# RWKV-7 front of a decoder trunk: decay and rate ranks as column pairs from unmixed input, keys first, two wide POOL products on VectorE

## What is computed

```python
xx = jnp.pad(h[:, :-1], ((0, 0), (1, 0), (0, 0))) - h
mixed = h[None] + xx[None] * mu[:, None, None, :]
r, k, v = jnp.einsum('ibsd,ide->ibse', mixed[:3], w_rkv)
xw, xa, xg = mixed[3], mixed[4], mixed[5]
w_log = -jax.nn.softplus(-(w_dec0 + jnp.tanh(xw @ w_dec1) @ w_dec2).astype(f32)) - 0.5
decay = jnp.exp(-jnp.exp(w_log))
a = jax.nn.sigmoid((a0 + (xa @ a1) @ a2).astype(f32))
g = jax.nn.sigmoid(xg @ g1) @ g2
kk = heads(k * k_k)
kk = kk / jnp.maximum(jnp.sqrt(jnp.sum(kk * kk, axis=-1, keepdims=True)), 1e-12)
k_h = heads(k) * (1.0 + (a_h - 1.0) * k_a.astype(f32).reshape(RW_HEADS, RW_HEADSIZE))
o = rwkv7_scan(r_h, w_h, k_h, v_h, kk, a_h)
```

## Time and profile before

| | |
|---|---|
| time, three runs | 1217.82 us median (1216.81 to 1221.8) |
| profiled execution | 1216.76 us, its span 1215.0 us |
| mean granted TensorE clock | 0.969 |
| TensorE busy | 1150.2 us, 95% |
| VectorE busy | 431.4 us, 36% |
| ScalarE busy | 267.9 us, 22% |
| POOL busy | 93.5 us, 8% |

### The profile page before, as it was taken

The page is one execution under the profiler, slowest core; times in us unless marked ns, Lnnn a source line. Parts: engine busy times, 40 slices in busy tenths (PEclk is TensorE's granted clock), DMA queues, the critical chain, the costliest instruction groups (busy, mean ns, idle before and its releaser), DMA issues.

```text
span 1215.0 us, 15687 instructions
## 1 busy us (share of the span) xinstructions
PE 1150.2 (95%) x6523; PEld 762.4 (63%) x6523; DVE 431.4 (36%) x946; ACT 267.9 (22%) x439; POOL 93.5 (8%) x106
## 2 busy tenths in 40 slices
PE   4799999998989999999999799979999999999997
PEld 2686698984478844444445478838887844444455
DVE  0364654265720321111111484874423411111113
ACT  2222010414220311111111353323331311111113
POOL 5002221200000100000000001331000100000000
PEclk9899899999989899999999899998988999999999
DMA  9797765329967379959999630000069689999991
GB/s 352 262 331 276 277 229 187 138 98 381 402 238 266 121 292 385 387 201 369 387 386 340 246 104 35 1 0 2 2 218 390 223 306 386 387 387 386 387 383 42
DMA packets 157180, 309.56 MB, mean 255 GB/s; under 512 B 9568, under 2 KB 10940, under 8 KB 157116
## 3 DMA queue, kind: packets, MB, share of 16 engines
q1 hardware_dynamic: 156320, 307.39, 69.5%
q10 hardware_dynamic: 796, 1.23, 0.3%
HBM read 307.55 MB, written 1.05 MB: 254 GB/s over the span
## 4 chain that ended last, share of the span: by engine, by line
PE 86%; DVE 6%; SPq 2%; ACT 2%; DMA 1%; issue 1%; ACTq 1%; DVEq 0%
PE bank L1136 19%; PE bank L779 15%; PE bank L1160 10%; PE bank L840 7%; PE bank L1069 6%; PE bank L1061 6%; PE bank L790 2%; PE bank L906 2%; DVE scratch L2406 2%; PE bank L812 1%; PE bank L749 1%; PE bank L1193 1%; PE bank L1201 1%; PE bank L1372 1%; DVE scratch L2408 1%
## 5 line engine op out<-in xcount | busy, mean ns | idle before, releaser
L779 PE MATMUL bank<-arena,ring 128*128 128x256 f32 x960 | 211.5, 382 | 5.5 <-DMA ring<-in_ev_w_in 2.8
L779 PEld LDWEIGHTS bank<-arena,ring 128*128 128x128 f32 x960 | 182.8, 191 | 30.8 <-DMA ring<-in_ev_w_in 3.2
L1136 PE MATMUL bank<-ring,arena 128*64 128x512 f32 x704 | 153.7, 592 | 0.0
L1136 PEld LDWEIGHTS bank<-ring,arena 128*64 128x64 f32 x704 | 50.4, 137 | 99.6 <-issue 99.4
L2280 DVE TENSOR_TENSOR arena<-arena,bank 128x512 f32<-128x512 f32 x17 | 11.7, 688 | 220.7 <-PE bank L1136 220.7
L840 PE MATMUL bank<-arena,ring 128*128 128x256 f32 x384 | 86.1, 388 | 2.8 <-DVE arena L2504 2.8
L1069 PE MATMUL bank<-arena 128*128 128x256 f32 x336 | 83.1, 394 | 1.7 <-issue 1.7
L1136 PE MATMUL bank<-arena 128*64 128x512 f32 x384 | 84.1, 592 | 0.0
L840 PEld LDWEIGHTS bank<-arena,ring 128*128 128x128 f32 x384 | 74.8, 195 | 14.0 <-issue 3.2
L1061 PEld LDWEIGHTS bank<-arena 128*128 128x128 f32 x608 | 69.3, 192 | 13.8 <-issue 13.8
L1061 PE MATMUL bank<-arena 128*128 128x128 f32 x608 | 72.7, 278 | 0.0
(11 more groups left out here) (358 smaller groups left out, 1337.4 us busy)
## 6 DMA issues: line engine op xcount, KB each, us to landing
ring<-in_moe_w SPq DMA_DIRECT2D x112, 1024.0 KB, 14.2
arena<-in_moe_w SPq DMA_DIRECT2D x80, 1024.0 KB, 14.2
ring<-in_mod_w SPq DMA_DIRECT2D x24, 2048.0 KB, 11.0
ring<-in_ev_w_in SPq DMA_DIRECT2D x13, 2048.0 KB, 12.8
ring<-in_od_w_rkv SPq DMA_DIRECT2D x6, 2048.0 KB, 13.6
ring<-in_ev_w_out SPq DMA_DIRECT2D x4, 2048.0 KB, 17.1
ring<-in_od_w_o SPq DMA_DIRECT2D x2, 2048.0 KB, 10.7
arena<-in_x ACTq DMA_DIRECT2D x1, 1024.0 KB, 9.1
```

The costliest lines, as they stand in the source:

```text
L779: mm = pe.matmul(ps[:, c * S:(c + 1) * S], w_cols(slot)[:, k, (2 * half + c) * P:(2 * half + c + 1) * P], src[:, k, :], start=(k == 0), st ...
L1136: mm = pe.matmul(bank[4 + half][e * C:(e + 1) * C, :], hgT[:, kb, e * C:(e + 1) * C], piece(slots[e], kb), start=(kb == 0), stop=(kb == KB ...
```

## The change

- Decay and rate ranks: POOL scales the two 64-wide first weights with mu once their tile has landed. TensorE computes `h @ w + xx @ (mu * w)` for both, side by side in the two column halves of bank 4, one rank in partitions 0 to 63 and one in 64 to 127. The second products read row halves 0 to 63 and 64 to 127 and go to two banks (`decay_and_rate`). Their mixed inputs are no longer made; VectorE makes the four differences and mixes gate, key, receptance and value.
- The gate's first product stands between the second and third `decay_and_rate`, its second product behind the key projections and lengths. Keys are projected next after the ranks. Two of the four `key_products` stand within the first receptance tile.
- ScalarE does all four key evacuations, then all four roots, then the gate, then LT. The value mix stands ahead of the maxima on VectorE, when the key projections are done.
- The receptance products (L724, L729) go from POOL to VectorE, behind the second transpose of the solve.

```diff
+    FULL_RANKS = FULL_IN + 8
...
-                    srcs = [(wt[0:64, 0:D], t["od_w_dec2"][0]), (wt[0:64, D:2 * D], t["od_a2"][0]),
-                            (wt[:, 2 * D:3 * D], t["od_g2"][0])]
+                    srcs = [(wt[0:64, 0:D], t["od_w_dec2"][0]), (wt[64:P, 0:D], t["od_a2"][0]),
+                            (wt[:, D:2 * D], t["od_g2"][0])]
...
-                    sp.wait_ge(lora_full, 3)
+                    sp.wait_ge(lora_full, 2)
...
-                    sp.wait_ge(proj_full, FULL_LORA)
+                    sp.wait_ge(proj_full, FULL_LORA + 4)
...
-                    sp.wait_ge(proj_full, FULL_LORA + 2 * at + 2)
+                    sp.wait_ge(proj_full, (FULL_LORA if at >= 2 else FULL_RANKS) + 2 * at + 2)
...
-            pool.wait_ge(proj_full, FULL_LORA + 4)
+            _, slot, count = plan[1][places[1, "la"][0]]
+            pool.wait_ge(tile_landed[slot], 16 * count)
+            for i in range(2):
+                for k in range(KB):
+                    v = (i * KB + k) * HEAD
+                    ins = pool.tensor_scalar(weight(slot)[:, 2048 + v:2048 + v + HEAD], weight(slot)[:, v:v + HEAD],
+                                             col("od_mu", (3 + i) * KB + k), None, ALU.mult)
+            ins.then_inc(ranks_scaled, 1)
+            pool.wait_ge(proj_full, FULL_RANKS + 4)
...
-            pool.memset(buf(11), 0.0)
-            pool.wait_ge(rw_exp, 4)
-            pool.wait_ge(proj_evac, 26 + 12 + 8)
-            pool.tensor_tensor(AR[:, :, :, 1, :], by_tile(5), by_tile(10), ALU.mult).then_inc(r_ready, 1)
+            pool.memset(buf(11), 0.0).then_inc(kc_ready, 1)
...
-                if pr == 1:
-                    pool.wait_ge(r_ready, 1)
-                    pool.tensor_tensor(by_tile(10), AR[:, :, :, 1, :], rwK, ALU.mult).then_inc(r_ready, 1)
...
-                second = [wl[0:64, 0:D], wl[0:64, D:2 * D], wl[:, 2 * D:3 * D]]
-                rank = [64, 64, P]
-                for i in range(3):
+                second = [wl[0:64, 0:D], wl[64:P, 0:D], wl[:, D:2 * D]]
+                low = [slice(0, 64), slice(64, P)]
...
+                scaled_first = [wa[:, 2048 + 512 * i:2560 + 512 * i].rearrange("p (k n) -> p k n", k=KB)
+                                for i in range(2)]
...
+                for k in range(KB):
+                    if k % 2 == 0:
+                        pe.wait_ge(h_ready, 8 + k // 2 + 1)
+                    for i in range(2):
+                        pe.matmul(bank[4][low[i], 0:S], first[i][:, k, :], hT[:, k, :], start=(k == 0), stop=False)
+                pe.wait_ge(ranks_scaled, 1)
+                for k in range(KB):
+                    if k % 2 == 0:
+                        pe.wait_ge(diff_ready, k // 2 + 1)
+                    for i in range(2):
+                        mm = pe.matmul(bank[4][low[i], 0:S], scaled_first[i][:, k, :], xx[:, k, :],
+                                       start=False, stop=(k == KB - 1))
+                mm.then_inc(lora_full, 1)
...
+                def decay_and_rate(u):
...
+                    two_banks = (proj_bank(), proj_bank())
+                    for c in range(2):
+                        d = 2 * u + c
+                        for i in range(2):
+                            mm = pe.matmul(two_banks[i][:, c * S:(c + 1) * S], second[i][:, d * P:(d + 1) * P],
+                                           lora[0][low[i], :], start=True, stop=True)
+                            if c:
+                                mm.then_inc(proj_full, 1)
...
+                def gate_first():
...
-                        pe.wait_ge(mix_ready, i + 4 if i else k // 2 + 1)
-                        mm = pe.matmul(bank[4][0:rank[i], 0:S], first[i][:, k, :], mixed[i % 2][:, k, :],
+                        if k % 2 == 0:
+                            pe.wait_ge(mix_ready, k // 2 + 1)
+                        mm = pe.matmul(bank[5][:, 0:S], first[2][:, k, :], mixed[0][:, k, :],
...
-                    pe.wait_ge(lora_evac, i + 1)
...
+                def gate_second():
...
-                            mm = pe.matmul(ps[:, c * S:(c + 1) * S], second[i][:, d * P:(d + 1) * P],
-                                           lora[i][0:rank[i], :], start=True, stop=True)
+                            mm = pe.matmul(ps[:, c * S:(c + 1) * S], second[2][:, d * P:(d + 1) * P], lora[1],
+                                           start=True, stop=True)
...
+                pe.wait_ge(lora_evac, 1)
+                decay_and_rate(0)
+                decay_and_rate(1)
+                gate_first()
+                decay_and_rate(2)
+                decay_and_rate(3)
...
+                    src = mixed[(1, 0, 1)[n]]
...
+                pe.wait_ge(mix_ready, 5)
+                rkv(0, 0)
+                rkv(0, 1)
+                pe.wait_ge(lora_evac, 2)
+                early_lengths()
+                late_lengths()
+                gate_second()
+                pe.wait_ge(mix_ready, 6)
...
+                def early_products():
+                    pe.wait_ge(kk_max, 4)
+                    key_products(0)
+                    key_products(1)
...
+                rkv(1, 0, between=early_products)
+                key_products(2)
+                key_products(3)
+                rkv(1, 1)
...
-                rkv(0, 0)
-                rkv(0, 1, early_lengths)
-                pe.wait_ge(mix_ready, 8)
-                rkv(1, 0, late_lengths)
-                pe.wait_ge(kk_max, 4)
-                for j in range(4):
-                    key_products(j)
-                rkv(1, 1)
-                pe.wait_ge(mix_ready, 9)
...
-                        pe.wait_ge(kc_ready, pr + 1)
+                        pe.wait_ge(kc_ready, pr + 2)
...
-                lora_func = [ACT.Tanh, ACT.Copy, ACT.Sigmoid]
-                for i, (dst, bias) in enumerate(((sgT, "od_w_dec0"), (aT, "od_a0"), (ggT, None))):
-                    r = P if i == 2 else 64
-                    act.wait_ge(lora_full, i + 1)
-                    act.activation(lora[i][0:r, :], bank[4][0:r, 0:S], lora_func[i]).then_inc(lora_evac, 1)
-                    for u in range(4):
+                act.wait_ge(lora_full, 1)
+                act.activation(lora[0][0:64, :], bank[4][0:64, 0:S], ACT.Tanh)
+                act.activation(lora[0][64:P, :], bank[4][64:P, 0:S], ACT.Copy).then_inc(lora_evac, 1)
+                for u in range(4):
+                    for dst, bias in ((sgT, "od_w_dec0"), (aT, "od_a0")):
...
-                        if bias is None:
-                            ins = act.activation(dst[:, 2 * u:2 * u + 2, :].rearrange("p k s -> p (k s)"),
-                                                 bank[n % 4][:], ACT.Copy)
-                        else:
-                            for c in range(2):
-                                b = 2 * u + c
-                                ins = act.activation(dst[:, b, :], bank[n % 4][:, c * S:(c + 1) * S], ACT.Sigmoid,
-                                                     bias=col(bias, b))
+                        for c in range(2):
+                            b = 2 * u + c
+                            ins = act.activation(dst[:, b, :], bank[n % 4][:, c * S:(c + 1) * S], ACT.Sigmoid,
+                                                 bias=col(bias, b))
...
+                act.wait_ge(lora_full, 2)
+                act.activation(lora[1], bank[5][:, 0:S], ACT.Sigmoid).then_inc(lora_evac, 1)
...
-                evac_keys(0)
-                evac_keys(1)
-                evac_keys(2)
-                key_root(0)
-                key_root(1)
-                evac_keys(3)
-                key_root(2)
-                key_root(3)
-                evac_products(0)
-                evac_products(1)
-                evac_T(rT, 0)
-                evac_products(2)
-                evac_products(3)
+                for u in range(4):
+                    evac_keys(u)
+                for u in range(4):
+                    key_root(u)
+                evac_T(ggT, 0)
+                evac_T(ggT, 4)
+                for j in range(4):
+                    evac_products(j)
...
+                evac_T(rT, 0)
...
-                    i = (3, 4, 5, 1, 0, 2)[n]
+                    i, place = ((5, 0), (1, 1), (0, 0), (2, 1))[n]
...
-                        if n == 0 and b % 2 == 0:
-                            tt_(xx[:, b:b + 2, 1:S], hT[:, b:b + 2, 0:S - 1], hT[:, b:b + 2, 1:S], ALU.subtract)
-                            link(ts_(xx[:, b:b + 2, 0:1], hT[:, b:b + 2, 0:1], -1.0, None, ALU.mult))
-                        ins = stt(mixed[n % 2][:, b, :], xx[:, b, :], col("od_mu", i * KB + b), hT[:, b, :],
+                        ins = stt(mixed[place][:, b, :], xx[:, b, :], col("od_mu", i * KB + b), hT[:, b, :],
...
-                dve.wait_ge(h_ready, 12)
+                for q in range(4):
+                    dve.wait_ge(h_ready, 8 + q + 1)
+                    b = 2 * q
```

(50 more changed lines are left out.)

## The result

The changed kernel takes 1209.3 us (median of 9 runs; before 1217.8, 9 runs). One of its nine runs took 2005.74 us at a granted clock of 0.553 and is left out of the ratio. The ratio is 0.9919, 95% interval 0.9896 to 0.9942: 0.8% faster.

The account below looks back on a forecast made before the run. It took two nearly equal paths, TensorE's stream and the solve, to bound the front. An earlier loop start (-5.8) and the clock (-3.0) gave -8.8 from 1216.76: 1208.0 profiled, 1209 as median, range 1204 to 1217.

Parts of the forecast that it names:

- What bounds: Layer 1's front: TensorE's stream (813.6) and the solve (820.2) end within 6.7 us of each other.
- Ranks: Decay and rate rank matmuls, paired in column halves: 0.11 us a record, keys start 12.1 us earlier.
- The feared half microsecond at the sigmoids: ScalarE's sigmoids keep ahead of the banks by only 0.2 us; half a microsecond may be lost there.
- The rival that pairs don't overlap: Rank pairs don't run side by side: 0.216 us a record, +6.8, 1215.8 us; chance 0.10.
- the rival of weight loads in the open: Weight loads of the rank column pairs don't overlap matmuls: 0.353 us a record, +15.6, 1224.7 us; chance 0.05.
- The new wait: TensorE stands 6.5 us before the first receptance tile, until the gate copy behind four key roots; half clock costs 2.7 more.
- Part 3: Receptance products moved from POOL to VectorE: worth 5.8 us of the 8.4 us that two solve steps stood still.
- the first two parts: Part 1: paired decay and rate ranks, keys 12.1 us earlier. Part 2: keys first, loop may start 5.8 us earlier.
- The clock at the loop: Idle before the loop shrinks from 6.7 to 0.7 us, so its first pass keeps full clock: 3.0 us gained, at most 4.0.
- Sum: -5.8 for the loop's earlier start and -3.0 for the clock make -8.8: 1208.0 profiled, 1209 median.

Follow-up runs that it names:

- products_alone: The kernel before with only the two wide receptance products moved from POOL to VectorE, behind the second transpose; 1209.70 us, ratio 0.9929 to the kernel before.
- ranks_apart: The changed kernel with all matmuls of the decay rank ahead of all of the rate rank in both accumulations; 1213.25 us, ratio 0.9961 to the kernel before.
- gate_early: The changed kernel with the gate's four evacuations between ScalarE's second and third key root; 1199.94 us, ratio 0.9857 to the kernel before.
- fill_wait: The changed kernel with 13 idle matmuls on TensorE between the gate's second product and the first receptance tile; 1207.01 us, ratio 0.9900 to the kernel before.
- pool_back: The changed kernel with the two wide receptance products left on POOL; 1215.63 us, ratio 0.9985 to the kernel before.
- fill_loop: The kernel before with 14 idle matmuls between TensorE's last projection and the wait for the solve; 1214.98 us, ratio 0.9962 to the kernel before.
- early_pool: The changed kernel with the gate evacuated between the second and third key root and the receptance products back on POOL; 1206.64 us, ratio 0.9898.

## Why the prediction was right

The forecast was 1209, the measurement 1209.3. The mechanism was right; that the number agrees to 0.3 us is luck, as the ratio's interval is 2.8 us wide either way. Step by step:

- **What bounds.** Two paths that end close together, TensorE's stream and the solve: shown. products_alone shortens only the solve and takes the whole 6 us; ranks_apart lengthens only TensorE's stream and loses 4.6.
- **Ranks.** 0.11 us a record was predicted, 0.113 came. From first matmul to last end I had 9.7 us; it was 8.5, because the clock came back 2.9 us after work resumed and not 5.5. Keys start 23.8 us after the norm's sums; the forecast was 24.8. The feared half microsecond at the sigmoids was 0.15. The rival that pairs don't overlap fell: 0.113 a record in pairs, 0.216 from start to start within one rank in ranks_apart. So did the rival of weight loads in the open: the 32 loads of the second accumulation take 3.39 us within its matmuls' 3.63. The sentence of the Trainium skill (TensorE: Matmul & The Clock Gate, Packing small matmuls) that a weight load overlaps running matmuls only if its row group differs does not hold here, where both halves use the same rows.
- **The new wait.** 6.5 us forecast, 6.25 measured; 2.7 forecast for the half clock after it, 3.1 measured by gate_early and by fill_wait. Its cause is shown, not only argued: four instructions moved into an idle spell of ScalarE remove it.
- **Part 3.** I gave it 5.8 of 8.4 us, with ScalarE's copies ending 3.5 us ahead of the loop's start; the last of them (L1857) ends at 802.95, 6.7 ahead of it. The term that was off is the solve's start, which I had no earlier than before: two of the four LT products now come 9 us ahead of the others, so half of the masks (758.72, 8 of 16) are done early, and the masks end 89.8 us after the norm's sums for 92.8. So without part 3 the first two parts were not worth nothing: the front of pool_back is 2.3 us shorter than before, and part 3 is worth the other 3.9 us of front and 2.0 at the clock.
- **The clock at the loop.** 3.0 forecast. The loop's first pass is 2.6 shorter in the change, and 2.6 in fill_loop, where only the matmuls ahead of the loop were added: the term was 0.4 too high. From the second L1356 to the third, and on to the fourth, it takes the same 17.4 us in all ten profiles. That hand-offs to VectorE keep it from 4.0 is argued, not shown.
- **Sum.** -5.8 and -3.0 were forecast, -6.2 and -2.6 came. Two small errors cancel; inside the 6.2 the keys came 1.0 earlier than forecast and the wait was 0.25 shorter, and the half clock after it cost 0.4 more.

So the first two parts, for all their 13 us at the ranks, are worth only 0.0010 in the timed ratio (the change against products_alone) or 0.0015 (pool_back against the kernel before), both within the intervals. Their gain was given back at once, in the moved gate product, the wait behind four roots and the clock. With the wait removed they show: gate_early against products_alone is 0.7%.

## What to carry to other kernels

When the profile shows two paths that end within a few microseconds, cost both to their ends before a change; a gain on one is worth only the difference, and an instruction that holds the other (a wide POOL product beside a chain of small dependent VectorE steps) can be the cheapest edit of all. When work is moved ahead of a stage, follow the buffers: a bank whose evacuation is queued behind another chain turns into a wait, and the wait of 6.25 us here also brought TensorE's clock down, which added half of the wait again (3.1 us). Compare two profiles by stretches between instructions that the change leaves alone, since code that is the same moved by up to 9 us from one profile to the next.

## What the runs showed of the hardware

Between the norm's sums and the loop's start the ten profiles have 15 spells of 2.96 to 7.07 us in which TensorE did nothing. After every one of them the clock was at 1.2 GHz when work resumed. In the ranks and projections it was back 2.7 to 6.2 us after work resumed, at the loop's start 8.1 us and, in pool_back, 6.7.

In early_pool TensorE was idle for 4.09 us ahead of the loop, and the clock then stayed at 1.2 GHz for some 17 us, from about 811.2 to 828.2. Its windows:

```profile
811.00:820.00 9.00, 8.37 (x118) 6.62 (x119) 3.87 (x12) 2.99 (x9) 1.18 (x2) 0.51 0.01 2
820.00:828.00 8.00, 8.00 (x49) 6.12 (x48) 2.91 (x8) 1.21 (x4) 0.65 (x2) 0.50 0.01 2
828.00:830.00 2.00, 2.00 (x44) 1.85 (x45) 0.00 (x0) 1.64 (x6) 0.53 (x1) 0.94 0.00 0
```

TensorE counts as busy nearly throughout (8.37 of 9 us, then all 8). pool_back has the same idle spell (4.06 us) ahead of the same matmuls, and there the first pass lost 2.0 us to the clock, not 6.5. So the length of an idle spell and the work behind it don't settle what it costs; what does is not shown. The long spell at half clock is in one profile; how often it goes so was not tried.

The wide POOL products held a VectorE step each time: in the four kernels that have them on POOL (before, pool_back, fill_loop, early_pool) the eight products took 4.50 to 4.72 us, and beside each of them one solve step took 4.57 to 4.68 us for its usual 0.39 to 0.41.
